# Expert gates of tokens 0 to 127: one-hot products replaced by accumulating indirect transfers

## The reference

```
q = (x @ w_q), 8 heads, two halves of 128
s1, i1 = top 16 of the first half's scores over 128 keys;  s2, i2 likewise
top 16 of the 256 sums s1 + s2;  expert e = 128 * i + j
gate = softmax over those 16
y[t] = sum over heads and 16: gate * gelu(u[e] . x[t]) * v[e]
```

## Time and profile before

| | before |
|---|---|
| Median of 3 runs | 2553.51 us (2549.29 to 2554.78) |
| Span of the profiled execution (its own time; no other is listed) | 2553.6 us |
| PE matmuls busy | 2458.0 us, 96% |
| DVE busy | 1790.3 us, 70% |
| ACT busy | 1207.0 us, 47% |
| POOL busy | 265.6 us, 10% |
| DMA | 483.66 MB, mean 189 GB/s |

### The profile page before, as it was taken

One profiled execution on the slowest core, in us unless ns is written; L12 is line 12 of the kernel. 1 busy time (PEld: TensorE's weight loads), 2 busy tenths in 40 slices (PEclk: granted clock), 3 DMA queues, 4 the chain that ended last, 5 costly groups with the idle time before them and its releaser, 6 DMA issues.

```text
span 2553.6 us, 41919 instructions
## 1 busy us (share of the span) xinstructions
PE 2458.0 (96%) x16535; PEld 2233.5 (87%) x16535; DVE 1790.3 (70%) x3178; ACT 1207.0 (47%) x1803; POOL 265.6 (10%) x124
## 2 busy tenths in 40 slices
PE   7998999999999999988999999999999899999999
PEld 7867999999988888777999999988888788787997
DVE  5576696888766677756696888766767667555675
ACT  4344445444555554444445455455454564435433
POOL 0000485000000000000485000000000102000000
PEclk9999999999999999989999999999999999899999
DMA  7544587666677777542587666677777542143655
GB/s 233 172 128 149 186 228 221 192 187 188 197 244 265 241 235 244 167 127 97 181 230 223 188 188 191 193 247 255 245 239 244 185 132 91 62 138 124 182 163 176
DMA packets 201426, 483.66 MB, mean 189 GB/s; under 512 B 24080, under 2 KB 93712, under 8 KB 200720
## 3 DMA queue, kind: packets, MB, share of 16 engines
q1 hardware_dynamic: 197920, 473.46, 59.7%
q10 hardware_dynamic: 3312, 7.53, 0.9%
HBM read 446.30 MB, written 34.60 MB: 188 GB/s over the span
## 4 chain that ended last, share of the span: by engine, by line
PE 87%; DVE 8%; ACT 2%; issue 1%; DMA 1%; ACTq 0%; SPq 0%; DVEq 0%
PE psum L1019 29%; PE psum L1065 26%; PE psum L817 22%; PE psum L1042 4%; DVE rounded L1524 2%; PE psum L1183 2%; ACT rounded L2576 1%; DMA sb<-in_ret_w_in 1%; PE psum L1000 1%; PE psum L949 1%; DVE sb L1559 0%; DVE sb L1580 0%; PE psum L1149 0%; PE psum L1151 0%; PE psum L1442 0%
## 5 line engine op out<-in xcount | busy, mean ns | idle before, releaser
L1524 DVE TENSOR_TENSOR rounded<-sb,rounded 128x1024 fp32r<-128x1024 f32 (+3 forms) x696 | 813.9, 1172 | 548.8 <-ACT rounded L2959 322.4
L2959 ACT ACTIVATE rounded<-sb 128x1024 fp32r<-128x1024 f32 x512 | 543.0, 1061 | 758.6 <-PE psum L1019 361.8
L1019 PE MATMUL psum<-rounded 128*128 128x256 f32 x6144 | 767.4, 284 | 0.0
L1019 PEld LDWEIGHTS psum<-rounded 128*128 128x128 f32 x6144 | 743.6, 191 | 0.0
L1065 PE MATMUL psum<-rounded,weights 128*128 128x512 f32 x3072 | 698.1, 389 | 2.0 <-DVE weights L2506 1.7
L1065 PEld LDWEIGHTS psum<-rounded,weights 128*128 128x128 f32 x3072 | 576.2, 188 | 123.3 <-issue 2.9
L817 PE MATMUL psum<-rounded 128*128 128x256 f32 (+1 forms) x3924 | 590.0, 312 | 32.5 <-DVE rounded L1524 20.9
L817 PEld LDWEIGHTS psum<-rounded 128*128 128x128 f32 x3924 | 540.5, 194 | 78.3 <-DVE rounded L1524 22.3
L2576 ACT ACTIVATE rounded<-sb 128x1024 fp32r<-128x1024 f32 (+4 forms) x280 | 265.7, 954 | 396.1 <-PE psum L817 283.6
L790 POOL TENSOR_TENSOR rounded<-sb,rounded 128x1024 fp32r<-128x1024 f32 x96 | 237.5, 2479 | 484.5 <-ACT rounded L2959 484.0
L2497 DVE TENSOR_TENSOR halves<-halves,small 128x768 bf16<-128x768 bf16 x256 | 131.5, 555 | 4.4
(11 more groups left out here) (388 smaller groups left out, 1475.3 us busy)
## 6 DMA issues: line engine op xcount, KB each, us to landing
sb<-in_u_turned SPq DMA_DIRECT2D x256, 512.0 KB, 3.9
sb<-in_peer_v SPq DMA_DIRECT2D x256, 512.0 KB, 3.5
hidden<-sb SPq DMA_DIRECT2D x256, 128.0 KB, 3.9
sb<-hidden SPq DMA_DIRECT2D x256, 128.0 KB, 3.3
sb<-in_ret_w_in SPq DMA_DIRECT2D x48, 512.0 KB, 3.9
sb<-in_ffn_w_up SPq DMA_DIRECT2D x40, 512.0 KB, 4.0
sb<-in_peer_w_q SPq DMA_DIRECT2D x32, 512.0 KB, 3.8
sb<-in_ffn_w_down SPq DMA_DIRECT2D x22, 512.0 KB, 4.2
```

The source lines that it names most:

```text
L1019: mm = pe.matmul(ps(bank, 1)[:, 0:T], u[p][:, k * P:(k + 1) * P], hT[:, q, k, :], start=(k == 0 and w == 0), stop=(k == KD - 1 and w == 2))
L1524: vec.tensor_tensor(ring_lo[0:k, part, 0:wide], ring[0:k, slot, 0:wide], ring_hi[0:k, part, 0:wide].bitcast(F32), ALU.subtract).then_inc(c ...
L2959: act.activation(ring_hi[:, n % SPLIT, :], ring[:, n % RING, :], ACT.Copy).then_inc(tile_hi, 1)
```

## The change

Tokens 128 to 255 keep the groups: 32 of 4 tokens, five groups over twelve tiles (`g * 12 // 5`). Tokens 0 to 127 get their gates through memory. For each peer phase there is a block `gates` of 128 x 128 x 128 numbers in HBM (8 MB). POOL clears it by eight stores of 1 MB from a tile of zeros, one behind every fifth of its 48 splits. DVE works out, for each token, head and choice, the place (128 j + i) 128 + t. When POOL has made its splits, it adds the gates by indirect transfers with an adding operation, each with one number per partition (token): sixteen per head, 128 in all, and before the next head it waits until the sixteen have landed. Then it loads the block into the first half of G by eight transfers of 1 MB, each with its own semaphore, and DVE waits for a part before it multiplies the first of the part's 16 tiles. G is laid out as two halves of 128 tokens, which are walked as two runs.

```diff
-GROUPS = T // 4
+GROUPS = P // 4
+ZERO = 2048
+PARTS = NK * P // ZERO
...
+def by_half(ap):
+
+    return ap.rearrange("p (b t) -> p b t", b=TB)
...
+        gates_kept = [nc.dram_tensor(f"gates{l}", (P * NK * P, 1), F32, kind="Internal").ap() for l in range(2)]
...
-                a["G"] = m.take(NK, T)
+                a["G"] = m.take(TB, NK, P)
...
-            group_after.setdefault(FIRST_GROUP + g * 6 // 5, []).append(g)
+            group_after.setdefault(FIRST_GROUP + g * 12 // 5, []).append(g)
...
+            def pool_peer(phase, a):
+                l, nth = int(phase[4]), peers_before[phase]
+                by_row = gates_kept[l].rearrange("(j e) one -> j (e one)", j=P)
+                gp.wait_ge(phase_done, phases.index(phase))
+                gp.memset(a["zero"], 0.0).then_inc(*own.next())
+                for i in range(BY_POOL):
+                    n = begin[phase + "_u"] + i
+                    gp.wait_ge(tile_hi, tile_count[n])
+                    gp.tensor_tensor(ring_lo[:, n % SPLIT, :], ring[:, n % RING, :], ring_hi[:, n % SPLIT, :].bitcast(F32),
+                                     ALU.subtract).then_inc(pool_split, 1)
+                    if i % 5 == 4 and i // 5 < PARTS:
+                        if i == 4:
+                            done()
+                        gp.dma_start(by_row[:, i // 5 * ZERO:(i // 5 + 1) * ZERO], a["zero"]).then_inc(gates_blank, 16)
+                gp.wait_ge(gates_blank, 16 * PARTS * (nth + 1))
+                gp.wait_ge(places_known, nth + 1)
+                place = a["place"].bitcast(U32)
+                for hd in range(PH):
+                    if hd:
+                        gp.wait_ge(head_added, 16 * TOPK * (PH * nth + hd))
+                    for k in range(TOPK):
+                        gp.indirect_dma_start(gates_kept[l], bass.IndirectOffsetOnAxis(place[:, hd, k:k + 1], 0),
+                                              a["ijg"][:, 2, 0, hd, k:k + 1], None, compute_op=ALU.add).then_inc(head_added, 16)
+                gp.wait_ge(head_added, 16 * TOPK * PH * (nth + 1))
+                gp.wait_ge(onehots_made, gates_before[phase] + 1)
+                for n in range(PARTS):
+                    per = NK // PARTS
+                    gp.dma_start(a["G"][:, 0, n * per:(n + 1) * per, :].rearrange("p i t -> p (i t)"),
+                                 by_row[:, n * ZERO:(n + 1) * ZERO]).then_inc(gates_loaded[n], 16)
...
                     for w in range(3):
-                        for tb in range(TB):
-                            mm = pe.transpose(ps(0, 2)[:, w * T + tb * P:w * T + (tb + 1) * P],
-                                              a["ijg"][:, w, tb, :, :].rearrange("p a b -> p (a b)"), ident)
+                        mm = pe.transpose(ps(0, 2)[:, w * T:w * T + P], a["ijg"][:, w, 1, :, :].rearrange("p a b -> p (a b)"), ident)
...
                 vec.tensor_tensor(gate, gate, bcast(den, 2, TOPK), ALU.mult).then_inc(*own.mark(vec_for_pe))
+                vec.tensor_tensor(a["rest"][:, 0, 0:P], ident, iota, ALU.mult).then_inc(*own.next())
+                done()
+                lane, spot = a["rest"][:, 1, 0:1], a["abf"][:, 0]
+                vec.tensor_reduce(lane, a["rest"][:, 0, 0:P], AX, ALU.add).then_inc(*own.next())
+                vec.scalar_tensor_tensor(spot, a["ijg"][:, 1, 0], float(NK), a["ijg"][:, 0, 0], ALU.mult, ALU.add).then_inc(*own.next())
+                done()
+                vec.tensor_scalar(a["place"].bitcast(U32), spot, float(P), lane, ALU.mult, ALU.add).then_inc(*own.mark(places_known))
+                done()
...
-                        vec.tensor_copy(routes[:, w, :], ps(0, 1)[:, w * T:(w + 1) * T]).then_inc(*own.next())
...
+                        vec.tensor_copy(routes[:, w, 0:P], ps(0, 1)[:, w * T:w * T + P]).then_inc(*own.next())
...
                 def apply_gates(i):
                     vec.wait_ge(hid_loaded[i % 4], loaded_by(d0, i))
-                    vec.tensor_tensor(G[:, i, :], G[:, i, :], hid_back[:, i % 4, :], ALU.mult).then_inc(*own.mark(multiplied))
+                    if i % (NK // PARTS) == 0:
+                        vec.wait_ge(gates_loaded[i // (NK // PARTS)], 16 * (peers_before[phase] + 1))
+                    vec.tensor_tensor(G[:, :, i, :], G[:, :, i, :], by_half(hid_back[:, i % 4, :]), ALU.mult).then_inc(*own.mark(multiplied))
...
-                    act.activation(G[:, :, 4 * g:4 * g + 4], ps(4 + g % 2, 1).rearrange("p (q i) -> p i q", q=4),
+                    act.activation(G[:, 1, :, 4 * g:4 * g + 4], ps(4 + g % 2, 1).rearrange("p (q i) -> p i q", q=4),
...
-                    if i == NK + 24:
-                        act.wait_ge(weights_ready, d0 + 16)
+                    if i == NK + 28:
+                        act.wait_ge(weights_ready, d0 + 26)
                         load_params(phase)
```

More of the change, by code:

```diff
@@ L397, in build @@
         gates_placed = sem("gates_placed")
+        gates_blank, places_known, head_added = sem("gates_blank"), sem("places_known"), sem("head_added")
+        gates_loaded = [sem(f"gates_loaded{n}") for n in range(PARTS)]
         gelu_done, multiplied = sem("gelu_done"), sem("multiplied")
@@ L483, in build @@
                 l = int(phase[-1])
-                a["G"] = m.take(NK, T)
+                a["G"] = m.take(TB, NK, P)
                 up = arena()
                 up.take(2, D)
+                a["ijg"], a["place"], a["zero"] = up.take(3, TB, PH, TOPK), up.take(PH, TOPK), up.take(ZERO)
                 a["keys"], a["qT"] = up.take(2, SLOT), up.take(HC, T)
@@ L491, in build @@
                 a["s2"], a["cand"], a["cand2"] = up.take(HC, NK), up.take(PH, TOPK * TOPK), up.take(PH, TOPK * TOPK)
-                a["sel"] = up.take(PH, TOPK, TOPK)
                 a["val"], a["idx"], a["idxf"] = (up.take(HC, TOPK) for _ in range(3))
@@ L495, in build @@
                 a["ab"], a["abf"] = up.take(2, PH, TOPK), up.take(2, PH, TOPK)
-                a["ijg"], a["den"] = up.take(3, TB, PH, TOPK), up.take(TB, PH)
+                a["den"] = up.take(TB, PH)
                 a["rest"] = up.take(2, T)
@@ L787, in _ @@
                 if phase.startswith("peer"):
[L788 to L791, removed]
+                    pool_peer(phase, A[phase])
                 if phase == "mixers":
@@ L2471, in take_routes @@
                     for w in range(2):
-                        vec.tensor_copy(routes[:, w, :], ps(0, 1)[:, w * T:(w + 1) * T]).then_inc(*own.next())
-                    g = ps(1, 1)[:, 0:T]
-                    vec.tensor_copy(routes[:, 2, :], g).then_inc(*own.next())
+                        vec.tensor_copy(routes[:, w, 0:P], ps(0, 1)[:, w * T:w * T + P]).then_inc(*own.next())
+                    g = ps(1, 1)[:, 0:P]
+                    vec.tensor_copy(routes[:, 2, 0:P], g).then_inc(*own.next())
                     done()
-                    vec.tensor_tensor(rest[:, 0, :], g, routes[:, 2, :], ALU.subtract).then_inc(*own.mark(vec_served))
+                    vec.tensor_tensor(rest[:, 0, 0:P], g, routes[:, 2, 0:P], ALU.subtract).then_inc(*own.mark(vec_served))
                     done()
-                    vec.tensor_copy(routes[:, 3, :], rest[:, 0, :]).then_inc(*own.next())
+                    vec.tensor_copy(routes[:, 3, 0:P], rest[:, 0, 0:P]).then_inc(*own.next())
                     done()
-                    vec.tensor_tensor(rest[:, 1, :], rest[:, 0, :], routes[:, 3, :], ALU.subtract).then_inc(*own.next())
+                    vec.tensor_tensor(rest[:, 1, 0:P], rest[:, 0, 0:P], routes[:, 3, 0:P], ALU.subtract).then_inc(*own.next())
                     done()
-                    vec.tensor_copy(routes[:, 4, :], rest[:, 1, :]).then_inc(*own.next())
+                    vec.tensor_copy(routes[:, 4, 0:P], rest[:, 1, 0:P]).then_inc(*own.next())
                     done()
@@ L2501, in apply_gates @@
                     vec.wait_ge(hid_loaded[i % 4], loaded_by(d0, i))
[L2502 removed]
+                    if i % (NK // PARTS) == 0:
+                        vec.wait_ge(gates_loaded[i // (NK // PARTS)], 16 * (peers_before[phase] + 1))
+                    vec.tensor_tensor(G[:, :, i, :], G[:, :, i, :], by_half(hid_back[:, i % 4, :]), ALU.mult).then_inc(*own.mark(multiplied))
                 def weigh(i):
                     vec.wait_ge(weights_hi, d0 + i + 1)
[L2506 removed]
+                    vec.tensor_tensor(by_half(tile_w[:, i % 3, 1, :]), G[:, :, i, :], by_half(tile_w[:, i % 3, 0, :]).bitcast(F32),
                                       ALU.subtract).then_inc(*own.mark(weights_ready))
@@ L2980, in weigh @@
                         act.wait_ge(chunks_done, first_v + i - 2)
-                    act.activation(tile_w[:, i % 3, 0, :], G[:, i, :], ACT.Copy).then_inc(weights_hi, 1)
+                    act.activation(by_half(tile_w[:, i % 3, 0, :]), G[:, :, i, :], ACT.Copy).then_inc(weights_hi, 1)
                 hi_to(end[phase + "_q1"])
```

1 line of the change is left out of this document (removed).

## The result

The changed kernel takes 2643.14 us (median of 4 runs, 2638.32 to 2646.03) against 2551.40 for the kernel before beside it (4 runs, 2548.58 to 2554.78): ratio 1.035, 95% interval 1.0335 to 1.0365, so 3.5% slower. 2514 was foretold, at most 2630. The profiled span is 2640.4 us, 86.8 above the one before.

A forecast was written before the change was run, and what follows sets the result against it. PE was taken to bound both parts of u, and v. From a 2553.6 us span, -48 groups, -2 routes, +4 clearing and +6 loading back gave 2514 us; own range 2500 to 2535, with rivals 2500 to 2630.

The forecast's parts named there:

- The groups: Second part of u: 32 fewer gate groups in each of two peer phases, 0.75 us each, -48 us.
- the routes: One-hot routes half as wide, so PE waits less for the first one-hots: 1 us a phase, -2 us.
- Rival C: Something else holds u at 3.46 us a tile, so the gain doesn't come: about 2562 us; chance 0.02.
- The issue of the scatter: POOL's 128 indirect transfers a phase at 1.2 us each, done 67 us before v needs them: 0.
- The window of 252 us: Time for the scatter, from POOL's 48th split at 426.6 to v's first product, less the first load and multiply.
- the landings: POOL's waits for each head's sixteen transfers: 3.9 us, eight times, 31 us a phase.
- rival A: Each issue waits behind a DVE split, 2.43 us; scatter 90 us late in each phase: 2694 us; chance 0.29.
- Clearing: Eight 1 MB stores a phase in u's first part, 0.25 us each, +4 us; bounds 0 to 42 us.
- Loading back: 8.4 MB a phase issued at once in the last part of u, 3 us a phase, +6 us.
- rival B: Stores and loads both cost their bound of 42 us, PE standing while they pass: 2588 us; chance 0.09.
- The edits at nothing: Changes priced at 0, among them the extra place instructions on DVE and walking G in two runs in v.
- The places: Four more DVE instructions, at most 1.7 us, covered by DVE's 6.05 us wait for ACT: 0.

The follow-up runs named there:

- half_spread: Changed kernel with 8 of 16 choices per head scattered, loads of G six tiles apart, clearing in 32 stores of 256 KB from SP's queue: 2510.61 us, ratio 0.9829.
- micro_issue: Separate kernel, none of the reference's work: sections of 16 indirect issues on POOL, alone, not adding, on fewer partitions or beside VectorE work; adding issue alone 1.56 us.
- full_spread: Changed kernel with clearing in 32 stores of 256 KB from SP's queue, all 128 adding issues and the load in one go kept: 2622.94 us, ratio 1.0267.
- half_paced_load: Changed kernel with 8 of 16 choices scattered, eight clearing stores before the first u tile, loads of G issued six tiles apart: 2524.13 us, ratio 0.9883.
- half_early: Changed kernel with 8 of 16 choices per head scattered and all eight clearing stores issued before the first u tile: 2549.11 us, ratio 0.9983.
- half_scatter: Changed kernel with only the first 8 of 16 choices per head scattered, 64 issues a phase, stores and loads unchanged: 2546.88 us, ratio 0.9983.
- full_plain: Changed kernel with 128 issues that write without adding, clearing in 32 small stores from SP's queue, loads of G spaced: 2523.66 us, ratio 0.9884.

## Why the prediction was wrong, point by point

**The groups: right.** 64 groups at 0.75 us and the routes, -50 us. In the window from 560 to 680 the trace has 903 hidden products, 37.6 tiles of 24, so 3.19 us a tile as foretold; a phase gained 25.1 us; half_spread came out 44 below the kernel before with the rest of the transfers still to pay. Rival C is out.

**The issue of the scatter: the step that failed.** "I take 1.2 us" stands in the trace at 2.17. The window of 252 us was read rightly, down to the first load of G (5.3 us from issue to DVE, 5.8 taken); the landings cost less than the 31 us allowed (45.6 / 2 = 23 for seven of them, 1.8 for the last). But 128 x 2.17 = 278, and the scatter began at 438.5, not 426.6: 8.5 of that by the clearing, 2.2 by a later start of u, 1.3 between the last split and the first issue. What this decides was in the text: 1.89 as the break-even and 2.48 as the upper end. The mechanism is rival A's, the late scatter, at a smaller size: 49.65 us a phase for 90. Its reason holds in part. Beside VectorE's f32 splits an issue is longer, by 0.27 on average and not by a whole split; the two-input work that the prediction named as excepted is what lengthens it, in micro_issue and in this kernel. The larger miss is that the instruction takes 1.56 by itself, and 0.34 to the next, which no row of before had. The value was chosen by the row of another kind of instruction (arithmetic on 512 columns) and by the middle of the two ends, and 0.60 was then set on the side of the break-even on which that middle lay. With ends of 0.33 and 2.48 and a limit at 1.73, nothing in the trace spoke for such a share.

**Clearing: +4 foretold, some 16 measured** between the first and the 48th split (8.5 and 7.1); by runs it is 21 (the changed kernel against full_spread) or 14 (half_paced_load against half_spread), each above what 32 small stores cost. The slack of 2.7 us of a single tile was compared with a single store at full rate; but a store's packets share the engines with several loads of the ring. From 300 to 438 us ACT waits for loads 39 times, 65.6 us in all, where the earlier trace rows has 16 times and 25.1 from 300 to 427:

```profile
ACT rounded L3004 <- DMA sb<-in_u_turned: 65.6, 39, 4.3
```

That makes 1.1 us a store in the first phase, 0.4 of the upper bound of 2.6.

**Loading back: +6 foretold, 25 measured where it falls into u** (half_early against half_paced_load). "The ring's loads take longer than 3.9 us" was seen, but priced by the stretch from 780 on, where a few loads run beside the stream. Eight megabytes issued at once delay a load to 17.87 us, past any slack of a tile. In the changed kernel itself they fall into v's start instead and cost 7.8 us there. So rival B's mechanism was there as well, with some 39 of its bound of 84 us (half_early against half_spread, 0.9983 - 0.9829): in half_scatter, where the scatter is early, the stores and the loads eat nearly the whole gain. Had an issue taken the 1.2 us foretold, the kernel would by that have come out near 2547, not at 2514, by an estimate from half_scatter, which has half the issues and packets: the forecast would have been wrong without A too.

**The edits at nothing: right.** The halves of G cost v nothing: half_spread's PE is busy all of the time from 720 to 760:

```profile
720.00:760.00 40.00, 40.00 (x178) 33.11 (x178) 27.95 (x46) 20.38 (x30) 0.00 (x0) 1.00 0.80 269
```

The places' two widest instructions took 2.17 and 2.46 us, not 0.42, beside POOL's last splits, and the second ends with them, at 437.33 against 437.24; in full_plain POOL waits 1.4 us for them, once.

**The range** ended at 2630, short of the time, since it never added A and B. By the prediction's own sum an issue of 2.17 us makes the scatter 128 x 2.17 + 31 = 309 us, 57 late, twice, which is 2628 and just inside; what the clearing and the loads cost beyond their terms comes on top. They were written as rivals, each with the other at its forecast; here both came.

## What to carry to other kernels

Work that is moved onto an idle engine has a deadline, and its number of instructions times their step has to be measured against it first; where the trace doesn't have the instruction, time sixteen of it by themselves before building the rest, or give each side of the break-even its share of the range. Bulk transfers beside a stream that feeds the bound engine are to be issued in small pieces and spaced by the stream's progress: the clearing and the loads cost some 39 us more in one go (half_early) than by the piece, and by the piece half_spread came within 6 us of the 50 that its groups and routes should give. Terms that fail independently are added in the range, not weighed against each other.

## What the runs showed of the hardware

- An adding indirect issue from POOL costs mostly by the instruction: 1.32 us with 32 addresses, 1.56 with 128. Plain writing takes 0.59 less (0.97), on POOL itself.
- Adding makes more packets: 2304 for 16 issues of 128 addresses, where plain writing makes 512.
- Which VectorE work lengthens an adding issue differs: two f32 inputs in SBUF 2.22 us, an f32 copy 1.87, two bf16 inputs or one input in PSUM 1.57 and 1.55.
- The other way round, in the changed kernel's timeline, two VectorE instructions on 128 x 128 numbers ran 2.17 and 2.46 us while POOL split a tile:

```profile
432.67 2.17 DVE L2501 SCALAR_TENSOR_TENSOR sb<-sb 128x128 f32<-128x128 f32 x1
...
434.87 2.46 DVE L2503 TENSOR_SCALAR sb<-sb 128x128 uint32<-128x128 f32 x1
```

- Beside eight transfers of 1 MB issued together by POOL, loads of 512 KB on SP's queue took up to 16.17 and 17.87 us, where they take 4.6 in the median.
- TensorE's granted clock was 0.50 (1.2 GHz) at the end of a pause of 50 us, and 0.74 in the 20 us in which it began again. The first 48 products behind the pause took 13.03 us, 0.27 each, where the earlier trace rows has 1230 in 280 us, 0.23 each, so that a pause costs somewhat more than itself.
